# Two-block transformer kernel: branch products moved ahead of the value products in the second scan, value products as three fp32r products, state gate's sigmoid inside its PSUM bank

## The reference, cut to what matters

```
(s_z, s_xbc, s_dt, g_q, g_f, g_i, g_g, m_q, m_k, m_v, m_i, m_f, m_o, gates) = split(u @ w_in)
y_ssd = ssd_branch(...)      y_hg = hgrn2_branch(...)      y_ml = mlstm_branch(...)
gate = sigmoid(gates)
merged = gate[0] * (y_ssd @ w_br_ssd) + gate[1] * (y_hg @ w_br_hg) + gate[2] * (y_ml @ w_br_ml)
h = h + merged @ w_out
```

## Time and profile before

| | |
|---|---|
| median of 3 runs | 2111.43 us (2110.57 to 2112.22) |
| profiled execution: span from the first to the last instruction | 2109.8 us |
| profiled execution: time of its own outside the span | not given by the profile; its span is 1.6 us under the median |
| TensorE busy | 1957.3 us, 93% |
| VectorE busy | 1269.6 us, 60% |
| ScalarE busy | 929.9 us, 44% |
| mean granted TensorE clock | 0.975 of full |

### The profile page before, as it was taken

How to read it: one execution, slowest core, us unless ns; L and a number is a source line. 1 busy time by engine, 2 the same in 40 slices (tenths; PEclk the granted TensorE clock), 3 DMA queues, 4 the chain that set the end, 5 groups by cost and what they waited for, 6 DMA issues and landing times. The chain is left out here.

```text
span 2109.8 us, 48527 instructions
## 1 busy us (share of the span) xinstructions
PE 1957.3 (93%) x20900; PEld 1693.1 (80%) x20900; DVE 1269.6 (60%) x2179; ACT 929.9 (44%) x1160; POOL 31.4 (1%) x62
## 2 busy tenths in 40 slices
PE   8999999999999999999999999999999887776766
PEld 7998869999999999988689999999977654443433
DVE  5888879488688568796895796786534311111111
ACT  5544655574565455556464754664422211111001
POOL 0000000000000000000000000000000000000000
PEclk9999999999999999999999999999999998888888
DMA  6555344455455554554444544555785999999997
GB/s 237 176 209 180 137 160 142 170 184 186 166 188 186 205 183 162 209 205 145 160 141 142 199 178 164 185 186 189 261 348 221 394 417 422 422 422 422 422 422 322
DMA packets 71791, 499.43 MB, mean 237 GB/s; under 512 B 8416, under 2 KB 8544, under 8 KB 13264
## 3 DMA queue, kind: packets, MB, share of 16 engines
q1 hardware_dynamic: 66528, 480.75, 59.7%
q0 software_dynamic: 4528, 15.28, 2.2%
q10 hardware_dynamic: 576, 1.05, 0.2%
HBM read 495.90 MB, written 1.15 MB: 236 GB/s over the span
## 5 line engine op out<-in xcount | busy, mean ns | idle before, releaser
L2646 DVE TENSOR_TENSOR ring_r<-ring,weights_and_u_split 128x2048 fp32r<-128x2048 f32 x88 | 201.4, 2291 | 76.6 <-ACT weights_and_u_split L1983 72.8
L1023 PE MATMUL bank<-weights_and_u_split,ring_r 128*128 128x256 f32 x1880 | 246.3, 283 | 0.0
L1023 PEld LDWEIGHTS bank<-weights_and_u_split,ring_r 128*128 128x128 f32 x1880 | 234.8, 192 | 0.0
L1018 PE MATMUL bank<-weights_and_u_split,hidden_and_weights_high 128*128 128x256 f32 x1664 | 211.4, 284 | 0.0
L1613 PE MATMUL bank<-arena 128*32 128x256 f32 x1552 | 129.6, 465 | 85.4 <-DMA arena<-stream 82.9
L1018 PEld LDWEIGHTS bank<-weights_and_u_split,hidden_and_weights_high 128*128 128x128 f32 x1664 | 203.6, 192 | 4.8 <-issue 4.3
L1983 ACT ACTIVATE weights_and_u_split<-ring 128x2048 fp32r<-128x2048 f32 x88 | 167.7, 1907 | 53.5 <-PE bank L1023 41.4
L3006 DVE COPY arena<-bank 128x128 f32<-128x128 f32 x32 | 9.3, 291 | 291.1 <-PE bank L1631 291.1
L1613 PEld LDWEIGHTS bank<-arena 128*32 128x32 f32 x1552 | 55.5, 126 | 152.1 <-issue 118.4
L2646 DVE TENSOR_TENSOR ring_r<-ring,hidden_and_weights_high 128x2048 fp32r<-128x2048 f32 x64 | 146.1, 2285 | 28.7 <-ACT hidden_and_weights_high L1983 28.6
L2151 ACT ACTIVATE arena<-bank 64x256 f32<-64x256 f32 x32 | 12.1, 377 | 341.9 <-PE bank L1613 341.9
(11 more groups left out here) (490 smaller groups left out, 3562.9 us busy)
## 6 DMA issues: line engine op xcount, KB each, us to landing
ring<-stream SPq DMA_DIRECT2D x323, 1024.0 KB, 4.9
arena<-stream SPq DMA_DIRECT2D x127, 1024.0 KB, 26.2
arena<-rows_scratch POOLq DMA_DIRECT2D x48, 256.0 KB, 4.2
place_of_rows<-stream SPq DMA_DIRECT2D x2, 1024.0 KB, 6.2
place_of_parameters<-stream SPq DMA_DIRECT2D x2, 1024.0 KB, 7.5
u<-stream SPq DMA_DIRECT2D x2, 1024.0 KB, 11.3
h<-x_d ACTq DMA_DIRECT2D x4, 256.0 KB, 5.1
out<-arena SPq DMA_DIRECT2D x2, 512.0 KB, 3.1
```

The source lines that it names most:

```text
L1018: pe.matmul(bank[:, c * S:(c + 1) * S], whi[k][:, c * P:(c + 1) * P], yhi[k] if xx is None else xx[:, k, :], start=(sub == 0 and c == part ...
L1023: mm = pe.matmul(bank[:, c * S:(c + 1) * S], wlo[k][:, c * P:(c + 1) * P], yhi[k] if xhi is None else xhi[:, k, :], start=False, stop=(end ...
L2646: tt(scan_high_or_low(k, ring_r[:, POS[k] % RING, :]), scan_high_or_low(k, w), high(k).bitcast(F32), ALU.subtract)\
```

## The change

The order of the units becomes `mq`, `mk`, `bs`, `mv`, `mo`, `gs`: `bs` in turns 8 to 11, `mv` in 12 to 15, `mo` in 16 to 19, `gs` in 20 to 23. `mv` becomes a split unit with three fp32r products; `hi` and `lo` now stand in every turn from 11 to 23. Since `bs` comes first, ScalarE copies its bank to MERGED, and at `gs` ScalarE takes the sigmoid inside the PSUM bank and VectorE multiplies the bank into MERGED. The gate bank is thus read by both. `u_low` waits for the last `mk` in place of the last `mv`; the item `msig` (sigmoid of the output gate) moves from turn 16 to turn 20. Some scratch places move with this (the high parts of the scan's units alternate between HF and Z, the small logs go to MVT), and the ones beside the values are set later.

```diff
-         + ["mq"] * 4 + ["mk"] * 4 + ["mv"] * 4 + ["mo"] * 4
-         + ["gs", "bs"] * 4 + ["gh"] * 4 + ...
+         + ["mq"] * 4 + ["mk"] * 4 + ["bs"] * 4 + ["mv"] * 4 + ["mo"] * 4
+         + ["gs"] * 4 + ["gh"] * 4 + ...
...
-SCAN = [... if kind in ("mo", "gs")] + [OF["gh"], OF["gh"] + 1]
+SCAN = [... if kind in ("mv", "mo", "gs")] + [OF["gh"], OF["gh"] + 1]
...
-        WSCAN = (HF, 122, HF, 122, HF, HF, HF, HF, 42, 0)
+        WSCAN = (HF, Z) * 6 + (42, 0)
...
         for i in range(2, 24):
-            if i in (17, 19, 21):
-                sched.append(("hi", gs + i - 15))
-            elif i == 23:
-                sched.append(("hi", gh))
-            elif 11 <= i <= 15:
-                sched.append(("hi", mo + i - 11 if i < 15 else gs))
+            if i >= 11:
+                sched.append(("hi", mq + i + 1))
...
-            if i == 16:
+            if i == 20:
                 sched.append(("msig", 0))
...  (the same for "lo")
+                    for part, (xx, wx) in enumerate(((uhi, whi), (uhi, wlo), (ulo, whi))):
+                        if part == 1:
+                            pe.wait_ge(wlo_ok.sem, wlo_ok.at(lay, NTH_SPLIT[n] + 1))
+                        elif part == 2 and n == OF["mv"]:
+                            pe.wait_ge(ulo_ok.sem, ulo_ok.at(lay, 2))
+                        for i in range(T):
+                            ...
+                            for k in range(4):
+                                mm = pe.matmul(G[use % GBANKS][:, :], xx[k][:, i * P:(i + 1) * P], wx[k], ...)
...
+                    if kind == "gs":
+                        act.activation(bank[:, :], bank[:, :], ACT.Sigmoid).then_inc(gs_sig.sem, 1)
+                        return
...
-                elif kind == "bs":
-                    dve.wait_ge(*evac(lay, n - 1))
+                elif kind == "gs":
+                    dve.wait_ge(*evac(lay, OF["bs"] + j))
                     tt(flat(MERGED + 2 * j, 2), bank[:, :], flat(MERGED + 2 * j, 2), ALU.mult).then_inc(f.sem, 1)
...
                 elif kind == "u_low":
-                    dve.wait_ge(unit_done.sem, unit_done.at(lay, POS[last("mv")] + 1))
+                    dve.wait_ge(unit_done.sem, unit_done.at(lay, POS[last("mk")] + 1))
```

More of the change, by code:

```diff
@@ L950, in unit @@
                     late = (n - OF["mv"]) % 2
[L951 to L958, removed]
+                    if high_at(n) == HF:
+                        wide = high(n).rearrange("p d (k m) -> p d k m", k=2)
+                        whi = [wide[:, k // 2, k % 2, :] for k in range(4)]
+                    else:
+                        wide = high(n).rearrange("p (k m) -> p k m", k=4)
+                        whi = [wide[:, k, :] for k in range(4)]
@@ new lines, in unit @@
+                    wide = ring_r[:, POS[n] % RING, :].rearrange("p (k m) -> p k m", k=4)
+                    wlo = [wide[:, k, :] for k in range(4)]
+                    uhi = [scan_u(4 * late + k, 1)[:, 0, :] for k in range(4)]
+                    ulo = [u_r[:, 4 * late + k, :] for k in range(4)]
+                    for part, (xx, wx) in enumerate(((uhi, whi), (uhi, wlo), (ulo, whi))):
[4 more added lines that the diff above has]
+                        for i in range(T):
+                            use = USE[n - late + i]
+                            if part == 0 and not late:
+                                pe.wait_ge(freed[use % GBANKS].sem, freed[use % GBANKS].at(lay, use // GBANKS))
+                            for k in range(4):
+                                if part == i == 0 and n < OF["mv"] + 2 and k % 2 == 0:
+                                    pe.wait_ge(uhi_ok.sem, uhi_ok.at(lay, 4 + 2 * late + k // 2 + 1))
+                                mm = pe.matmul(G[use % GBANKS][:, :], xx[k][:, i * P:(i + 1) * P], wx[k],
+                                               start=(not late and part == k == 0), stop=(late == 1 and part == 2 and k == 3),
+                                               skip_group_check=True)
@@ L1753, in unit @@
                 kind, j = KINDS[n], n - OF[KINDS[n]]
-                j = j // 2 if kind in ("gs", "bs") else j
-                if kind in ("rows", "bs", "bh", "bm", "out", "down") or kind in ("hi", "mv") and j % 2 == 0:
+                if kind in ("rows", "bh", "bm", "out", "down") or kind in ("hi", "mv") and j % 2 == 0:
                     return
@@ L2068, in _ @@
             act.wait_ge(lam_mm, 1)
-            act.activation(small[:, 2:4], A[3][:, 0:2], ACT.Exp).then_inc(lam_exp, 1)
+            act.activation(small[:, 2:4], A[3][:, 0:2], ACT.Exp).then_inc(yln.sem, 1)
             if upto == "ada":
@@ L2214, in unit @@
                 kind, j = KINDS[n], n - OF[KINDS[n]]
-                j = j // 2 if kind in ("gs", "bs") else j
-                if kind not in ("rows", "bs", "bh", "bm", "out", "down", "xbc", "up"):
+                if kind not in ("rows", "gs", "bh", "bm", "out", "down", "xbc", "up"):
                     return
```

53 lines of the change are left out of this document (26 added, 27 removed).

## The result

The changed kernel takes 2123.98 us (median; 2123.14 to 2128.07), the kernel before 2111.82 on the same chip: ratio 1.0057, 95% interval 1.0045 to 1.0068, so 12.2 us slower. I had said 2115.2, with 2119 as the upper end. The profiled execution took 2128.07 with a span of 2126.2; other executions of it had spans of 2121.3 to 2122.7. The lines of the code have moved. In the changed kernel L1217 has become L1227; L1228, L1237 and L1255 have become L1238, L1247 and L1265; the split units' L1018 and L1023 are L1028 and L1033, and `mv`'s L957 is L966. ScalarE's L1799, L1942 and L1983 are L1800, L1954 and L1993, VectorE's L2527 and L2646 are L2540 and L2659. The experts' matmuls, L1594, L1613, L1627 and L1647 before, are L1604, L1623, L1637 and L1657.

What follows compares the result with a forecast made beforehand. TensorE's work plus idle time bounds the layers, VectorE pacing the second scan. Per layer -5.9 +0.1 -1.36 +4.3 +2.6 +1.0 +0.5, plus 0.6 for `bs`, gives +1.9; twice, 3.8: 2115.2 us, own range 2112.5 to 2118, overall 2107 to 2119.

Steps and rivals of the forecast that it cites:

- VectorE sets the pace: Second scan, turns 14 to 18: VectorE's 7.40 us turn against TensorE's 6.65 makes TensorE wait 4.3 us, formerly 1.36.
- The square behind the `gs1` read: Turn 21: ScalarE's square queues behind the `gs1` read, so TensorE waits 2.6 us before the norm's sums.
- `gs3` behind the Exp: Turn 22: the high part of `gs3` runs behind the Exp, its low part behind VectorE's scaling; waits of 1.0 and 0.5 us.
- The sums and what follows keep their distances: Tail of the scan: after the square, spacing stays as before, `gs2` at +3.27 us, Ln at +3.66, Exp ending at +4.64.
- Nothing ahead of the experts idles long enough to take a delay back: From the layers to the experts: each layer's 1.9 us delay is passed on whole, 3.8 us in all.
- My walk: Turn-by-turn timeline of layer 0 from turn 12 to `gh`, repeated for layer 1: each layer ends 1.9 us later.
- A: Rival for the scan and its tail: VectorE's chain does not bind, the square finds time; full gain, 2096.8 us; 6%.
- B: Rival at turns 21 to 23: ScalarE squares before the `gs1` read; -2.3 us a layer, 2106.8 us; 12%.
- C: Rival at the mLSTM stage: `gh1` and `gh2` come later than TensorE's shift, another 1 to 2 us a layer, 2119; 12%.
- TensorE's busy time: Sign in the profile after: TensorE's total busy time falls by 12 us while the span grows.

Runs made afterwards that it cites:

- e1: The changed kernel with ScalarE's square for the branch norm moved ahead of the `gs1` read in turn 21; 2116.34 us, ratio 1.0013 to the kernel before.
- e2: As e1, with the high and low parts of `gs3` prepared ahead of `hnorm` again; 2114.01 us, ratio 1.0007 to the kernel before.
- b1: The kernel before, with ScalarE's square made to wait for the unit of turn 21 and one bank-sized copy; 2120.71 us, ratio 1.0038.
- b2: The kernel before, with ScalarE's square made to wait for the unit of turn 21 and four bank-sized copies; 2127.17 us, ratio 1.0075.
- a8: The changed kernel with 128 narrow unread instructions, half a packet, added at TensorE's start; 2118.78 us, ratio 1.0032 to the kernel before.
- e8: As e2, with 128 narrow unread instructions, half a packet, added at TensorE's start; 2109.54 us, ratio 0.9982 to the kernel before.

## Why the prediction was wrong

- **VectorE sets the pace** (new waits of 4.3 us): right. Waits 0.40, 0.93, 0.70, 0.70 and 1.14 sum to 3.87; turns of 7.40; the scan's end at 367.13 for my 367.0.
- **The square behind the `gs1` read** (2.6 us): right in mechanism and size, 2.48 in both layers, and e1 removes it by the square alone.
- **`gs3` behind the Exp** (1.0 and 0.5): 0.79 and 0.36; e2 shows it is the order.
- **"The sums and what follows keep their distances"**: the first step that failed. They did in layer 1 of the profile, which came to 1.84 a layer against my 1.9, and didn't in layer 0, where the sums took 3.2 us more at 1.2 GHz. I priced an idle stretch of 2.5 us as 2.5 us. Before, TensorE never idled at this point, so no row of it showed the clock there; b1 and b2 show it for the old order too, so it belongs to the wait and not to the new units.
- **"Nothing ahead of the experts idles long enough to take a delay back, and the expert loads hang on TensorE's own events, so both layers pass it on: 2 x 1.9 = 3.8 us"**: the second step that failed, and the larger. It is right about the delay and takes the rest for unchanged. It has no term for the length of TensorE's instruction stream. Half a packet more of instructions moved the late packets in the second block, and that cost 5.3 us (changed kernel against a8).
- **The sum.** e8 is 3.8 us under the kernel before. From it to a8, and again from e2 to the changed kernel, it is 10.6: 5.0 for the waits before the sums, 2.3 for the tail's order, and the 3.3 that are left put down to the clock. From e8 to e2, and again from a8 to the changed kernel, it is 5.3 for the packets. -3.8 + 10.6 + 5.3 = 12.1, and 12.0 by the ratio. My walk holds 3.7 of it (two times 1.84), the packets 5.3, the clock about 3. Each of these differences is good to 2 or 3 us, so that they meet so closely is in part luck.
- **The rivals.** A, the full gain, is out by the 7.40 and the waits in the trace. B, that the square doesn't wait, did not happen, but e8 builds it and puts the packets right: 3.8 us under the kernel before, where B was 4.6 under it. C had the direction for another reason; the mLSTM stage and what follows it in a layer added 0.4 us (4.87 at `gh`, 5.30 at the start of layer 1).
- **TensorE's busy time** was a poor sign. By the forecast's own sum it had to fall by 10.4 us, and not 12 (-5.9 + 0.1 + 0.6 a layer). In these profiles it rises, 1957.3 to 1959.6: the two scans lose 8.6 without the slowed sums, these add 3, and the experts' block, at a granted clock of 0.86 for 0.88, adds 7. In the second profiles it falls from 1966.5 to 1953.4.

## What to carry to other kernels

A stall on TensorE is priced with what comes behind it: ask for each new wait as long as the 2.5 us here what the clock does to the matmuls after it, and move an operation that others wait for ahead of a read that itself waits, even where it costs nothing on its engine. Where a long program runs into code that is bound by transfers, count the instructions that a change adds: read the stops without a releaser at the head of that code, see whether they end behind the landing of an instruction packet, and if they moved, shift them with a few narrow instructions in a covered place before you judge the change. And repeat such a test with a pad that is no multiple of the packet.

## What was not expected of the hardware

- After 2.5 us of idle time TensorE came back at half clock in 6 of 10 cases, after 4.1 us in 2 of 2, and in none of the 28 layers in which the same sums had no wait ahead of them. What decides between the 10 stays open.
- TensorE's instructions arrive in packets of 16384 bytes, 256 instructions, and in code of short matmuls (128 of them in 1.99 us) it stops for 1.2 to 4.6 us at bounds three packets apart or nearer; all 78 such stops end 1.2 to 1.7 us after a packet has landed. Why some bounds cost nothing is open. Where they fall was worth some 5 us in three pairs of programs.
- A GpSimd subtraction of 128x2048 takes 4.8 us, and a VectorE instruction of 0.69 us beside it 5.07.
